# Grid decay matrices from one fp32r product per head, with the clamped difference on ScalarE

## The chip, the core and the metric

The kernel runs on one core of a Trainium2 chip. The metric is device time in microseconds (us) of one execution; lower is better. Before the change it is 1022.42 us, the median of 3 runs (1021.97 to 1022.79).

## The reference

Three blocks run over 256 tokens of width 1024: an attention block with an MLP, a second one, and a hybrid block in which neighbourhood attention on a grid (8 heads) and a bidirectional state-space scan (8 heads, chunks of 128 tokens) run side by side. The change lies in the scan. For each direction and head it needs

```
cum = jnp.cumsum(dtc * a.reshape(g, e), axis=2)
seg = cum[:, :, :, None] - cum[:, :, None, :]
lower = np.tril(np.ones((q, q), dtype=bool))[:, :, None, None]
decay = jnp.exp(jnp.where(lower, seg, -jnp.inf))
cb = jnp.einsum("bcign,bcjgn->bcijg", cc, bc)
m = cb[..., None] * decay * dtc[:, :, None]
y_diag = jnp.einsum("bcijge,bcjgep->bcigep", m, xc)
```

`seg` is at most 0 where the mask holds, so the kernel computes exp(min(seg, 0)) and lets the masked `cb` remove the rest.

## The kernel before

All instruction streams are written by hand, one program per engine, and are tied by semaphores. The dense products (helper `product`, L681 to L683) are three fp32r matmuls each, on weights that ScalarE (L1374, `split_hi`) and VectorE (L1904, `split_lo`) split into high and low parts.

The change touches the grid stage, some 70 us long. There TensorE runs the list of `grid_order`, 16 window steps i (head i // 2, token half i % 2), with these pieces:

- S(i), L1216: the logits of step i in one of four small banks. VectorE adds the bias and takes the maximum (`window_logits`, L2561), ScalarE takes the exponential (L1763), VectorE scales by the reciprocal of the sum (`window_normalise`, L2567 and L2570).
- P(i), L690: four transposes of the probabilities; ScalarE copies them out (L1374, work<-bank 128x512). O(h), L1233: probabilities times values. After two heads ScalarE copies the pair's output (`pair_out`, acts<-bank 128x256), and VectorE makes its low part (`pair_lo`, L2574).
- G(h), L1239: head h's cumulative sums broadcast to 128 rows, into the segment bank, by a selector column of `ident` repeated 128 times against `cum_rows`, two fp32 products of 256 columns (one for each direction).
- `decay(h)`, L2591: VectorE makes min(row - column, 0) in four pieces (256, 128, 128 and 256 columns) from the segment bank into E[h % 2]. ScalarE takes the exponential of its 768 columns (L1769). `matrix(h)`, L2605: VectorE multiplies by dt and `cb`. GpSimd adds the overlapping parts (L657). Y(h), L1263, is the product with the values.
- F(n), L1252: the carried state's rows, also in the segment bank, read by `carried_rows` (L2619, L2623). K(1), L1246: transposed keys, in that bank too, copied out by ScalarE at step 2.

The one segment bank goes round in the order of SEGMENTS (G0 G1 K1 F0 G2 G3 F1 G4 G5 F2 G6 G7 F3), and each of these waits on `seg_free` of the one before. Each engine walks the 16 steps:

```
TensorE step i:  P(i), segments of step i, S(i+3), Y, O
ScalarE step i:  exp of S(i); exp of E if i-1 in DECAY; copy of P(i-1)
VectorE step i:  logits(i); normalise(i-1); carried rows; decay if i in DECAY; matrix if i-1 in DECAY
```

with DECAY = (1, 2, 4, 5, 7, 8, 10, 11). G(h) is issued two steps before its decay. After step 15 come the first product of the output projection, O(7), and the transposes T of the scan's rows. In step 12 (ScalarE) and 13 (VectorE) one weight chunk is split as well.

Before the stage, L1126 to L1130 compute the cumulative sums of all 16 rows (2 directions x 8 heads) in one bank, VectorE copies them to `cum` (L2507), and four transposes (L1137) give the columns in `stat` (L2511).

Of the kernel before, what the change touches and what calls it, by code (L numbers as in the profile page):

```python
# [215 lines left out]
def program(nc, weights, x_in, ctx_in, cols_in, rows_in, consts_in, pos_col_in, t5_pos_in, t5_cols_in, rpb_in, c_dram,  # L216
            final_dram, t5_dram, out):
    with ExitStack() as stack:
# [20 lines left out]
        posc = sbuf("posc", [P, 2], I32)  # L239
        post = sbuf("post", [P, 448], I32)  # L240
        t5c = sbuf("t5c", [P, 66])
        posf = sbuf("posf", [P, 2])
        rot = sbuf("rot", [P, 2, 2, 32])
        adac = sbuf("adac", [P, 80])
# [59 lines left out]
        cxsr = view(arena, 10752, 2, NA)  # L304
        Bcr = view(arena, 11776, 2, 2, P)
        cbm = view(arena, 12288, 2, 768)
        cum, cum_rows = arena[0:16, 13824:14336], arena[:, 13824:14336]
        tmp = lambda k: arena[:, 12288 + 64 * k:12352 + 64 * k]
        E = (work[:, 0:768], arena[:, 0:768])
        Wm = view(arena, 10752, 2, 768)  # L310
# [77 lines left out]
        conv_mid, conv_act = sem("conv_centre"), sem("conv_activated")  # L388
        sp_abs, sp_exp, sp_u, sp_ln = (sem("softplus_" + n) for n in ("abs", "exp", "one_plus", "ln"))
        a_exp, dA_ready, ecum_ready = sem("a_exp"), sem("dA_ready"), sem("exp_cum")  # L390
        xw_ready, seg_exp = sem("xw_ready"), sem("seg_exp")
        seg_ready, seg_free = sem("segment_ready"), sem("segment_free")
        y_ready, y_free = sem("state_rows_ready"), sem("state_rows_free")
# [50 lines left out]
        def window_unit(kind, i):  # L444
# [2 lines left out]

        seg_bank, y_banks, pair_bank = (gbank(GU["out"]), (gbank(GU["out"] + 1), gbank(GU["out"] + 2)),
                                        gbank(GU["out"] + 3))

        def segment_out(eng, kind, i):
            eng.wait_ge(seg_ready, SEGMENTS.index((kind, i)) + 1)
# [150 lines left out]
        @block.gpsimd  # L603
        def _(pool):

            pool.memset(half[:, :], -0.5).then_inc(pool_step, 1)
            pool.wait_ge(pool_step, 1)
            pool.memset(bias[:, 4096:4352], 0.0).then_inc(bias_zeros, 1)

            def roots(first, last):  # L610
                for n in range(first, last):
                    a, b = ROOTS[n]
                    pool.wait_ge(means_ready, n + 1)
                    pool.tensor_tensor(stat[:, a:b], stat[:, a:b], half[:, 0:b - a], ALU.pow).then_inc(roots_ready, 1)  # L614

            def ada_load(j, land):

                u = j % 2
                pool.dma_start(land[:, 2048 * u:2048 * u + 2048], weights["ada"][j]).then_inc(ada_in[u], 16)

            roots(0, 3)
            pool.wait_ge(roots_ready, 3)
            pool.memset(kpT[0][64:128], 0.0).then_inc(kpe_zeros, 1)
            pool.wait_ge(kpe_zeros, 1)
            pool.memset(kpT[1][0:64], 0.0).then_inc(kpe_zeros, 1)
            pool.wait_ge(kpe_zeros, 2)
            roots(3, 7)

            pool.wait_ge(act_lo, LO0["mlp0"] + 1)
            for j in range(2):  # L630
                ada_load(j, att)
            roots(7, 8)
            for j in range(2, 10):
                pool.wait_ge(ada_used, j - 1)
                ada_load(j, att)
            roots(8, 11)

            pool.wait_ge(act_lo, LO0["mlp1"] + 1)
            for j in (10, 11):
                ada_load(j, bias)  # L640
            roots(11, 12)
            for j in range(12, 24):
                pool.wait_ge(ada_used, j - 1)
                ada_load(j, bias)
            roots(12, 14)
            pool.memset(cum_rows, 0.0).then_inc(zeros_ready, 1)
            pool.wait_ge(zeros_ready, 1)
            pool.memset(nqT[0][64:128], 0.0).then_inc(zeros_ready, 1)
            pool.wait_ge(zeros_ready, 2)
            small_out(pool, SU["cb"] + 1)  # L650
            pool.memset(nqT[1][0:64], 0.0).then_inc(zeros_ready, 1)
            pool.wait_ge(zeros_ready, 3)
            for h in range(H):
                pool.wait_ge(w_mat, h + 1)
                diagonal, other = (bass.AP(Wm.tensor, Wm.offset + 768 * (h % 2) + a, [list(Wm.ap[0]), [256, 2], [1, P]])
                                   for a in (0, 384))
                pool.tensor_tensor(diagonal, diagonal, other, ALU.add).then_inc(w_summed, 1)  # L657
            roots(14, len(ROOTS))
# [3 lines left out]
        def _(pe):  # L662
# [457 lines left out]
            def cumulative():  # L1120

                pe.wait_ge(dA_ready, 1)
                u = SU["cum"]
                small_start(u)
                b = sbank(u)
                pe.matmul(b[0:16, 0:T], dA(0), const("upto"), start=True, stop=False)  # L1126
                pe.matmul(b[0:16, P:T], dA(1), const("upto", 0, P), start=False, stop=True)
                pe.matmul(b[0:16, T:2 * T], dA(1), const("since"), start=True, stop=False)
                pe.matmul(b[0:16, T:T + P], dA(0), const("since", P, P), start=False, stop=True).then_inc(small_ready, 1)

            def cumulative_columns():

                small_gone(pe, SU["cum"])
                u = SU["cumcol"]
                small_start(u)
                for n in range(4):
                    ins = pe.transpose(sbank(u)[:, 16 * n:16 * n + 16], cum[:, P * n:P * n + P], ident[0:16, 0:16])  # L1137
                ins.then_inc(small_ready, 1)
                u = SU["later"]
                small_start(u)  # L1140
                b = sbank(u)
                for n, (parts) in enumerate((
                        [("after", 0), ("ones", 1)], [("before", 0)], [("after", 1)], [("before", 1), ("ones", 0)])):
                    for m, (tri, t) in enumerate(parts):
                        ins = pe.matmul(b[:, 16 * n:16 * n + 16], const(tri), dA(2 + t), start=m == 0,
                                        stop=m == len(parts) - 1)
                ins.then_inc(small_ready, 1)
# [60 lines left out]
            def grid_work(kind, i):  # L1208
# [26 lines left out]
                        ins.then_inc(pair_ready, 1)  # L1235
                elif kind == "G":
                    segment_start(kind, i)
                    for d in range(2):
                        ins = pe.matmul(seg_bank[:, d * T:(d + 1) * T], repeated(ident, 8 * d + i, P),  # L1239
                                        cum_rows[:, d * T:(d + 1) * T], start=True, stop=True)  # L1240
                    ins.then_inc(seg_ready, 1)
                elif kind == "K":
                    segment_start(kind, i)
                    pe.wait_ge(nqk_ready, 3)
# [119 lines left out]
        def _(act):  # L1364
# [354 lines left out]
            used(GC["q"])  # L1719
            used(GC["q"] + 1)  # L1720
            small_gone(act, SU["cumcol"])
            act.activation(stat[:, 320:384], stat[:, 256:320], ACT.Exp).then_inc(ecum_ready, 1)
            u = SU["later"]
            small_out(act, u)
            act.activation(tmp(7), sbank(u)[:, 0:64], ACT.Exp).then_inc(small_free[u % 4], 1)
# [33 lines left out]
            for i in range(2 * H + 1):  # L1759
                if i < 2 * H:  # L1760
# [2 lines left out]
                    act.activation(att[:, 1024 + 512 * (i % 2):1536 + 512 * (i % 2)], sbank(u)[:, :], ACT.Exp, scale=-1.0,  # L1763
                                   bias=stat[:, 56 + i % 2:57 + i % 2], accum_out=stat[:, 60 + i % 2:61 + i % 2])\
                        .then_inc(small_free[u % 4], 1)
                if i - 1 in DECAY:
                    h = DECAY.index(i - 1)
                    act.wait_ge(seg_free, SEGMENTS.index(("G", h)) + 1)
                    act.activation(E[h % 2], E[h % 2], ACT.Exp).then_inc(seg_exp, 1)  # L1769
                if i == 1:  # L1770
                    context_keys(1)
                if i == 14:
# [78 lines left out]
        def _(v):  # L1851
# [652 lines left out]

            u = SU["cum"]
            small_out(v, u)
            v.tensor_copy(cum, sbank(u)[0:16, :]).then_inc(small_free[u % 4], 1)  # L2507
            used(GC["q"])
            u = SU["cumcol"]
            small_out(v, u)  # L2510
            v.tensor_copy(stat[:, 256:320], sbank(u)[:, 0:64]).then_inc(small_free[u % 4], 1)  # L2511
            used(GC["q"] + 1)
            rotate(0)
            rotate(1)
# [60 lines left out]
                                acts[:, 1, 0, p * T:(p + 1) * T].bitcast(F32), ALU.subtract)\  # L2575
                    .then_inc(pair_free, 1)

            parts = ((0, 256, 0, 0), (256, 384, 128, 1), (384, 512, 256, 0), (512, 768, 256, 1))

            def decay(h):  # L2580

                segment_out(v, "G", h)
                if h == 0:
                    for g in range(2):
                        small_gone(v, SU["cb"] + g)
                    small_gone(v, SU["cumcol"])
                if h >= 2:
                    v.wait_ge(w_mat, h - 1)
                for n, (a, e, src, t) in enumerate(parts):
                    c = 256 + 16 * t + h if n < 2 else 256 + 32 + 16 * t + 8 + h  # L2590
                    ins = v.tensor_scalar(E[h % 2][:, a:e], seg_bank[:, src:src + e - a], stat[:, c:c + 1], 0.0,  # L2591
                                          ALU.subtract, ALU.min)
                    if n == 3:
                        ins.then_inc(seg_free, 1)
                    else:
                        step(ins)
                settle()

            def matrix(h):
                v.wait_ge(seg_exp, h + 1)  # L2600
                if h >= 2:
                    v.wait_ge(y_used, h - 1)
                for n, (a, e, src, t) in enumerate(parts):
# [8 lines left out]
            def carried_rows(n):  # L2612
# [2 lines left out]
                tm = arena[:, 1024:1536]  # L2615
                v.wait_ge(ecum_ready, 1)
                segment_out(v, "F", n)
                c = 320 + 32 * d + 16 * t + 8 * d
                v.tensor_tensor(heads(tm), heads(seg_bank[:, :]), spread(stat[:, c:c + 8], 1, 64), ALU.mult)\  # L2619
                    .then_inc(seg_free, 1)  # L2620
                v.wait_ge(seg_free, SEGMENTS.index(("F", n)) + 1)
# [31 lines left out]
            for i in range(2 * H + 1):  # L2653
# [3 lines left out]
                    window_normalise(i - 1)  # L2657
                if i % 3 == 0 and 3 <= i <= 12:
                    carried_rows(i // 3 - 1)
                if i in DECAY:  # L2660
                    decay(DECAY.index(i))
                if i - 1 in DECAY:
                    matrix(DECAY.index(i - 1))
                if i == 13:
# [285 lines left out]
```

## Time and profile before

| what | value |
|---|---|
| median of 3 runs | 1022.42 us |
| profiled execution, first to last instruction | 1021.6 us |
| TensorE busy, whole span | 990.6 us (97%) |
| VectorE busy | 696.0 us (68%) |
| ScalarE busy | 512.6 us (50%) |
| mean granted TensorE clock | 0.996 |

The profiled execution is told by its span, 1021.6 us; the device time has a little more around it (0.8 us against the median). Times in the profile are counted from the span's start. The grid stage runs from 728.9 us (the first S) to about 800.9 us (the transposes T).

### The profile page before, as it was taken

Reading aid. Unit: us, or ns where it says so; the run is one execution under the profiler, and the core shown is the slowest. Engines: PE = TensorE matmul, PEld = TensorE weight load, DVE = VectorE, ACT = ScalarE, POOL = GpSimd, SP = SyncE. Lnnn points to the kernel's source line nnn. Section 1 sums busy time; section 2 is a strip of 40 time slices with the busy share of each in tenths; the row PEclk is TensorE's granted clock in tenths of the full one; section 3 lists DMA queues with packets and bytes.
Section 4 is the critical chain, followed back from the end, with each engine's and each line's share of the span. In section 5 each row is a group of like instructions: output and inputs, shape, how many; then the busy total and the mean of one; then the engine's idle time right before and its main releaser. Section 6 shows DMA issues by size and latency. Waiting matters only on the chain. (4 is left out here: it accounts for less than half of the span.)

```text
span 1021.6 us, 15144 instructions
## 1 busy us (share of the span) xinstructions
PE 990.6 (97%) x5976; PEld 860.0 (84%) x5976; DVE 696.0 (68%) x996; ACT 512.6 (50%) x687; POOL 48.3 (5%) x61
## 2 busy tenths in 40 slices
PE   7999999999989999999999999999998989999997
PEld 5577899999978877899998988988865779999996
DVE  5776647777775665657778564456598587777775
ACT  2366474544545665545454463544445354444443
POOL 0220000000000110000001010000010000000000
PEclk9999999999999999999999999999999999999999
DMA  9035576667664533568887543234101245545541
GB/s 363 16 101 147 206 278 222 249 249 277 230 223 141 192 122 115 215 250 326 293 326 285 211 163 115 92 124 165 42 1 42 104 164 192 185 185 184 187 177 42
DMA packets 29727, 183.92 MB, mean 180 GB/s; under 512 B 3440, under 2 KB 6128, under 8 KB 10096
## 3 DMA queue, kind: packets, MB, share of 16 engines
q1 hardware_dynamic: 25360, 157.56, 43.0%
q0 software_dynamic: 3456, 25.17, 6.7%
q8 instruction: 32, 0.52, 0.2%
q10 hardware_dynamic: 864, 0.55, 0.2%
q14 instruction: 15, 0.12, 0.0%
HBM read 180.64 MB, written 2.62 MB: 179 GB/s over the span
## 5 line engine op out<-in xcount | busy, mean ns | idle before, releaser
L1904 DVE TENSOR_TENSOR split<-raw,split 128x2048 fp32r<-128x2048 f32 (+1 forms) x123 | 279.9, 2275 | 203.5 <-ACT split L1374 202.2
L1374 ACT ACTIVATE split<-raw 128x2048 fp32r<-128x2048 f32 x122 | 231.8, 1900 | 248.3 <-PE bank L683 219.0
L681 PE MATMUL bank<-acts,split 128*128 128x256 f32 (+1 forms) x1024 | 290.8, 284 | 2.3 <-DVE acts L1944 1.4
L683 PE MATMUL bank<-acts,split 128*128 128x256 f32 (+1 forms) x1024 | 289.7, 283 | 0.0
L682 PE MATMUL bank<-acts,split 128*128 128x256 f32 (+1 forms) x1024 | 289.6, 283 | 0.0
L681 PE MATMUL bank<-split,acts 128*128 128x512 f32 (+1 forms) x544 | 211.4, 389 | 0.6 <-DVE split L1904 0.4
L682 PE MATMUL bank<-split,acts 128*128 128x512 f32 (+1 forms) x544 | 209.3, 385 | 0.0
L683 PE MATMUL bank<-split,acts 128*128 128x512 f32 (+1 forms) x544 | 209.1, 384 | 0.0
L681 PEld LDWEIGHTS bank<-acts,split 128*128 128x128 f32 (+1 forms) x1024 | 194.7, 190 | 6.0 <-DVE split L1904 1.9
L682 PEld LDWEIGHTS bank<-acts,split 128*128 128x128 f32 (+1 forms) x1024 | 194.7, 190 | 2.5 <-issue 0.2
L683 PEld LDWEIGHTS bank<-acts,split 128*128 128x128 f32 (+1 forms) x1024 | 194.7, 190 | 0.4
L683 PEld LDWEIGHTS bank<-split,acts 128*128 128x128 f32 x544 | 102.7, 189 | 20.5
L681 PEld LDWEIGHTS bank<-split,acts 128*128 128x128 f32 x544 | 102.7, 189 | 20.5 <-issue 1.0
L682 PEld LDWEIGHTS bank<-split,acts 128*128 128x128 f32 x544 | 102.9, 189 | 18.5
L1374 ACT ACTIVATE acts<-arena 128x1024 fp32r<-128x1024 f32 (+2 forms) x76 | 50.6, 689 | 47.8 <-DVE arena L2736 46.6
L614 POOL TENSOR_TENSOR stat<-stat,half 128x2 f32<-128x2 f32 (+4 forms) x18 | 25.4, 1409 | 435.4 <-DVE stat L1860 435.4
L2290 DVE CUSTOM_DVE_ANT_0 arena<-work,arena 128x1024 f32<-128x1024 f32 x36 | 43.9, 1220 | 0.7
L2290 DVE CUSTOM_DVE_ANT_0 arena<-bias,arena 128x1024 f32<-128x1024 f32 x28 | 34.2, 1221 | 1.0 <-DVE stat L1892 0.2
L681 PE MATMUL bank<-acts 128*128 128x512 f32 x88 | 34.6, 393 | 0.2 <-DVE acts L2697 0.2
L1821 ACT ACTIVATE arena<-bank,cols 128x256 f32<-128x256 f32 x22 | 12.4, 564 | 44.1 <-PE bank L683 44.1
L682 PE MATMUL bank<-acts 128*128 128x512 f32 x88 | 34.5, 392 | 0.0
L683 PE MATMUL bank<-acts 128*128 128x512 f32 x88 | 34.2, 389 | 0.0
(250 smaller groups left out, 1065.8 us busy)
## 6 DMA issues: line engine op xcount, KB each, us to landing
raw<-w_mlp SPq DMA_DIRECT2D x64, 1024.0 KB, 4.8
raw<-w_glu SPq DMA_DIRECT2D x22, 1024.0 KB, 4.8
bias<-w_ada POOLq DMA_DIRECT2D x14, 1024.0 KB, 6.8
raw<-w_qkv SPq DMA_DIRECT2D x12, 1024.0 KB, 4.7
arena<-w_glu_down SPq DMA_DIRECT2D x22, 512.0 KB, 3.3
work<-w_ada POOLq DMA_DIRECT2D x10, 1024.0 KB, 7.0
raw<-w_mla_o SPq DMA_DIRECT2D x4, 1024.0 KB, 5.8
raw<-w_moba_o SPq DMA_DIRECT2D x4, 1024.0 KB, 4.8
```

The source lines that it names most:

```text
L614: pool.tensor_tensor(stat[:, a:b], stat[:, a:b], half[:, 0:b - a], ALU.pow).then_inc(roots_ready, 1)
L681: pe.matmul(out_, a[0], b[0], start=first, stop=False)
L682: pe.matmul(out_, a[0], b[1], start=False, stop=False)
L683: return pe.matmul(out_, a[1], b[0], start=False, stop=last)
L1374: return act.activation(out_, in_, ACT.Copy)
L1821: act.activation(gact[:, b, :], gbank(u)[:, 0:T], ACT.Identity, scale=w, bias=bb).then_inc(glu_mid, 1)
L1904: v.tensor_tensor(split[:, c % 2, 1, 0:n], raw[:, c % 2, 0:n], split[:, c % 2, 0, 0:n].bitcast(F32), ALU.subtract).then_inc(lo_ready, 1)
L2290: ins = v.tensor_tensor_reduce(out=ada_junk[:, t, :], accum_out=modr[:, f:f + 1], scale=1.0, scalar=0.0, in0=(bias if layer else att)[:, 2 ...
```

## The change

Four things change. The 16 rows of cumulative sums become 8 rows with both directions in one row: columns 0 to 255 forward, 256 to 511 backward. The sums are split for fp32r: `cumr` rows 0 to 7 hold the rounded value, rows 32 to 39 what is left, and `pick` has ones at both places, so that one fp32r product of 512 columns adds the two and broadcasts a head's row. The clamped difference moves from VectorE to ScalarE, as Relu(column - row) in the same four pieces, and the exponential has scale -1. It moves from behind VectorE's normalise to behind ScalarE's exponential of the same step, and the exponential of E follows at once instead of one step later. VectorE's `decay` is gone.

```diff
-                pe.matmul(b[0:16, 0:T], dA(0), const("upto"), start=True, stop=False)
+                pe.matmul(b[0:8, 0:T], dA(0)[:, 0:8], const("upto"), start=True, stop=False)
...
-                    ins = pe.transpose(sbank(u)[:, 16 * n:16 * n + 16], cum[:, P * n:P * n + P], ident[0:16, 0:16])
+                    ins = pe.transpose(sbank(u)[:, 8 * n:8 * n + 8], cum[0:8, P * n:P * n + P], ident[0:8, 0:8])
...
                 elif kind == "G":
                     segment_start(kind, i)
-                    for d in range(2):
-                        ins = pe.matmul(seg_bank[:, d * T:(d + 1) * T], repeated(ident, 8 * d + i, P),
-                                        cum_rows[:, d * T:(d + 1) * T], start=True, stop=True)
-                    ins.then_inc(seg_ready, 1)
+                    if i == 0:
+                        pe.wait_ge(cum_parts, 1)
+                    pe.matmul(seg_bank[:, :], repeated(pick[:, :], i, P), cumr[:, :], start=True, stop=True)\
+                        .then_inc(seg_ready, 1)
...
-                if i - 1 in DECAY:
-                    h = DECAY.index(i - 1)
+                if i in DECAY:
+                    h = DECAY.index(i)
+                    segment_out(act, "G", h)
+                    if h >= 2:
+                        act.wait_ge(w_mat, h - 1)
+                    for n, (a, e, src, t) in enumerate(parts):
+                        c = 256 + 8 * t + h + 16 * (n // 2)
+                        ins = act.activation(E[h % 2][:, a:e], seg_bank[:, src:src + e - a], ACT.Relu, scale=-1.0,
+                                             bias=stat[:, c:c + 1])
+                    ins.then_inc(seg_free, 1)
                     act.wait_ge(seg_free, SEGMENTS.index(("G", h)) + 1)
-                    act.activation(E[h % 2], E[h % 2], ACT.Exp).then_inc(seg_exp, 1)
+                    act.activation(E[h % 2], E[h % 2], ACT.Exp, scale=-1.0).then_inc(seg_exp, 1)
...
-            v.tensor_copy(cum, sbank(u)[0:16, :]).then_inc(small_free[u % 4], 1)
+            v.tensor_copy(cum[0:8], sbank(u)[0:8, :]).then_inc(small_free[u % 4], 1)
+            small_gone(v, u)
+            step(v.tensor_tensor(pick[:, :], ident[:, 0:8], ident[:, 32:40], ALU.add))
+            step(v.tensor_copy(cumr[0:8, :], cum[0:8]))
+            settle()
+            v.tensor_tensor(cumr[32:40, :], cum[0:8], cumr[0:8, :].bitcast(F32), ALU.subtract).then_inc(cum_parts, 1)
...
-            def decay(h):
...
-                if i in DECAY:
-                    decay(DECAY.index(i))
```

ScalarE's order of instructions at steps 4 and 5, before (L1763 is the window's exponential, L1769 that of E, L1374 the copy of P):

```order
L1763 ACTIVATE work,stat<-bank,stat 128x512 [waits max_ready]
L1374 ACTIVATE work<-bank 128x4x128 [waits small_ready]
L1763 ACTIVATE work,stat<-bank,stat 128x512 [waits max_ready]
L1769 ACTIVATE work<-work 128x768 [waits segment_free]
L1374 ACTIVATE work<-bank 128x4x128 [waits small_ready]
```

The same steps now (L1769 is the window's exponential, L1779 the Relu pieces, L1783 the exponential of E, L1380 the copy):

```order
L1769 ACTIVATE work,stat<-bank,stat 128x512 [waits max_ready]
L1779 ACTIVATE work<-bank,stat 128x256 [waits mask_matrix_ready,segment_ready]
L1779 ACTIVATE work<-bank,stat 128x128 x2
L1779 ACTIVATE work<-bank,stat 128x256
L1783 ACTIVATE work<-work 128x768 [waits segment_free]
L1380 ACTIVATE work<-bank 128x4x128 [waits small_ready]
L1769 ACTIVATE work,stat<-bank,stat 128x512 [waits max_ready]
L1779 ACTIVATE arena<-bank,stat 128x256 [waits mask_matrix_ready,segment_ready]
```

Four Relu pieces and the exponential of E now stand between the window's exponential and the copy of the step before, in both steps.

TensorE's order at steps 3 and 4, before (L690 is P, L1239 is G, L1216 is S, L1263 is Y, L1252 is F):

```order
L1239 MATMUL bank<-arena,consts 128x256 [waits segment_free]
L1239 MATMUL bank<-arena,consts 128x256
L1216 MATMUL bank<-arena 128x512 [waits small_free0]
L1263 MATMUL bank<-arena 128x64 [waits mask_diagonals_summed]
L1263 MATMUL bank<-arena 128x64 x3
L690 MATMUL bank<-consts,work 128x128 [waits small_free1,probs_ready]
L690 MATMUL bank<-consts,work 128x128 x3
L1252 MATMUL bank<-work,arena 128x256 [waits segment_free]
```

The G of the same place now, and the S behind it:

```order
L1246 MATMUL bank<-cumr,pick 128x512 [waits segment_free]
L1222 MATMUL bank<-arena 128x512 [waits small_free0]
```

Two fp32 products became one of fp32r; nothing else of TensorE's order moved, and F(1) still waits for the segment bank that G(3) filled.

## Rows read from the trace of the kernel before

**Rows 1.** The page: busy us of each engine, its share of the span, instructions.

```profile
PE 990.6 (97%) x5976; PEld 860.0 (84%) x5976; DVE 696.0 (68%) x996; ACT 512.6 (50%) x687; POOL 48.3 (5%) x61
```

**Rows 2.** Window: busy us of PE, PEld, DVE, ACT, POOL; granted clock; DMA.

```profile
740.00:790.00 50.00, 46.23 (x233) 31.33 (x231) 44.10 (x125) 25.70 (x52) 5.81 (x8) 1.00 0.05 16
```

**Rows 3.** Waits of TensorE in 727 to 803 us: us in total, times, longest.

```profile
PE bank L690 <- DVE work L2570: 1.2, 2, 1.0
PE bank L1252 <- ACT arena L1374: 0.7, 1, 0.7
PE bank L1252 <- DVE arena L2591: 0.6, 1, 0.6
PE bank L1239 <- DVE work L2591: 0.6, 1, 0.6
PE bank L1216 <- ACT work L1763: 0.6, 1, 0.6
```

**Rows 4.** Timeline of TensorE: start us, us of the group, what, count.

```profile
744.62 1.03 PE L1239 MATMUL bank<-arena,consts 128*128 128x256 f32 x4
745.48 1.02 PE L1216 MATMUL bank<-arena 128*128 128x512 f32 x2
...
798.19 0.39 PE L681 MATMUL bank<-split,acts 128*128 128x512 f32 x1
798.42 0.39 PE L682 MATMUL bank<-split,acts 128*128 128x512 f32 x1
```

**Rows 5.** Timeline of VectorE where the sums are copied (684 to 690 us).

```profile
685.00 0.67 DVE L2507 COPY arena<-bank 16x512 f32<-16x512 f32 x1
687.37 2.29 DVE L1904 TENSOR_TENSOR split<-raw,split 128x2048 fp32r<-128x2048 f32 x1 [1.70 <-ACT split L1374]
```

**Rows 6.** ScalarE: three costs from PSUM (timeline, groups by form, timeline).

```profile
802.94 1.55 ACT L1375 ACTIVATE acts<-bank,cols 128x256 fp32r<-128x256 f32 x4
...
L1374 ACT ACTIVATE acts<-bank 128x256 fp32r<-128x256 f32 x4 | 1.5, 381 | 3.5 <-PE bank L1233 3.5
...
680.84 1.00 ACT L1713 ACTIVATE arena<-bank,cols 128x256 f32<-128x256 f32 x2
```

**Rows 7.** ScalarE: a line's durations in ns, min/median/max; L1763 has the bias as a column.

```profile
L1375 ACT ACTIVATE acts<-bank,cols x4: 456/471/482, 802.9 to 804.0; 128x256 fp32r<-128x256 f32 x4
...
L1763 ACT ACTIVATE work<-bank,stat x16: 678/687/691, 731.3 to 789.9; 128x512 f32<-128x512 f32 x16
```

**Rows 8.** Timeline of ScalarE around step 10.

```profile
767.39 0.84 ACT L1769 ACTIVATE arena<-arena 128x768 f32<-128x768 f32 x1
...
770.61 0.69 ACT L1763 ACTIVATE work<-bank,stat 128x512 f32<-128x512 f32 x1 [1.61 <-DVE stat L2561]
...
773.42 0.60 ACT L1374 ACTIVATE work<-bank 128x512 f32<-128x512 f32 x1 [2.03 <-PE bank L690]
```

**Rows 9.** The chain that ended last, 755 to 763 us: start us, us, what.

```profile
756.40 0.60 PE bank L690 x4
...
757.03 0.60 ACT work L1374
757.62 0.28 ACT acts L1374
...
757.93 0.43 DVE acts L2574
758.36 0.61 DVE bank L2561
...
759.48 1.39 DVE work L2591 x4
...
760.92 1.13 PE bank L1239 x4
```

**Rows 10.** Timeline of TensorE at the stage's end: P(15), and the transposes T.

```profile
792.85 0.66 PE L690 MATMUL bank<-consts,work 128*128 128x128 f32 x4
...
800.92 1.03 PE L690 MATMUL bank<-consts,work 128*128 128x128 f32 x8
```

More of the change, by code:

```diff
@@ L241, in program @@
         t5c = sbuf("t5c", [P, 66])
+        cumr = sbuf("cumr", [P, 512], F32R)
+        pick = sbuf("pick", [P, 8], F32R)
         posf = sbuf("posf", [P, 2])
@@ L306, in program @@
         cbm = view(arena, 12288, 2, 768)
-        cum, cum_rows = arena[0:16, 13824:14336], arena[:, 13824:14336]
+        cum = arena[0:16, 13824:14336]
         tmp = lambda k: arena[:, 12288 + 64 * k:12352 + 64 * k]
@@ L390, in program @@
         a_exp, dA_ready, ecum_ready = sem("a_exp"), sem("dA_ready"), sem("exp_cum")
+        cum_parts = sem("cum_parts_ready")
         xw_ready, seg_exp = sem("xw_ready"), sem("seg_exp")
@@ L449, in program @@
                                         gbank(GU["out"] + 3))
+        parts = ((0, 256, 0, 0), (256, 384, 128, 1), (384, 512, 256, 0), (512, 768, 256, 1))
         def segment_out(eng, kind, i):
@@ L645, in _ @@
             roots(12, 14)
-            pool.memset(cum_rows, 0.0).then_inc(zeros_ready, 1)
+            pool.memset(cumr[:, :].bitcast(F32), 0.0).then_inc(zeros_ready, 1)
             pool.wait_ge(zeros_ready, 1)
@@ L1125, in cumulative @@
                 b = sbank(u)
-                pe.matmul(b[0:16, 0:T], dA(0), const("upto"), start=True, stop=False)
-                pe.matmul(b[0:16, P:T], dA(1), const("upto", 0, P), start=False, stop=True)
-                pe.matmul(b[0:16, T:2 * T], dA(1), const("since"), start=True, stop=False)
-                pe.matmul(b[0:16, T:T + P], dA(0), const("since", P, P), start=False, stop=True).then_inc(small_ready, 1)
+                pe.matmul(b[0:8, 0:T], dA(0)[:, 0:8], const("upto"), start=True, stop=False)
+                pe.matmul(b[0:8, P:T], dA(1)[:, 0:8], const("upto", 0, P), start=False, stop=True)
+                pe.matmul(b[0:8, T:2 * T], dA(1)[:, 8:16], const("since"), start=True, stop=False)
+                pe.matmul(b[0:8, T:T + P], dA(0)[:, 8:16], const("since", P, P), start=False, stop=True)\
+                    .then_inc(small_ready, 1)
             def cumulative_columns():
@@ L1721, in _ @@
             small_gone(act, SU["cumcol"])
-            act.activation(stat[:, 320:384], stat[:, 256:320], ACT.Exp).then_inc(ecum_ready, 1)
+            act.activation(stat[:, 320:352], stat[:, 256:288], ACT.Exp).then_inc(ecum_ready, 1)
             u = SU["later"]
@@ L2510, in _ @@
             small_out(v, u)
-            v.tensor_copy(stat[:, 256:320], sbank(u)[:, 0:64]).then_inc(small_free[u % 4], 1)
+            v.tensor_copy(stat[:, 256:288], sbank(u)[:, 0:32]).then_inc(small_free[u % 4], 1)
             used(GC["q"] + 1)
@@ L2576, in pair_lo, with matrix @@
                     .then_inc(pair_free, 1)
-            parts = ((0, 256, 0, 0), (256, 384, 128, 1), (384, 512, 256, 0), (512, 768, 256, 1))
-            def decay(h):
-                segment_out(v, "G", h)
+            def matrix(h):
+                v.wait_ge(seg_exp, h + 1)
                 if h == 0:
@@ L2585, in decay @@
                         small_gone(v, SU["cb"] + g)
[L2586 to L2600, printed above, removed]
                 if h >= 2:
@@ L2617, in carried_rows @@
                 segment_out(v, "F", n)
-                c = 320 + 32 * d + 16 * t + 8 * d
+                c = 320 + 16 * d + 8 * t
                 v.tensor_tensor(heads(tm), heads(seg_bank[:, :]), spread(stat[:, c:c + 8], 1, 64), ALU.mult)\
```

## The prediction

> **What bounds the kernel now.** I read the page first: TensorE is busy for 990.6 of 1021.6 us [rows 1], so a saving must end up on TensorE's own path. Then the window of the stage that the change touches: in 50 us TensorE is busy for 46.2, VectorE for 44.1, ScalarE for 25.7 [rows 2]. So the stage is bound by TensorE with VectorE close behind, and ScalarE looks half free. Then TensorE's waits there: F(0) 0.7, F(3) 0.6 and G(5) 0.6 us for the segment bank, P(12) and P(14) 1.2 for the normalise, S(15) 0.6 for an exponential [rows 3]. They are short, but they show that the loop TensorE to ScalarE to VectorE and back takes about as long as TensorE's own work. Last the chain of waits from P(5) on [rows 9]: it leaves TensorE for ScalarE's copy, `pair_out`, VectorE's `pair_lo`, logits and decay, and comes back with G(5) at 760.92 us. This loop decides the case.
>
> **TensorE's term.** G is four passes: 744.62 to 745.48 us, 0.86 us [rows 4] (a group's first start to the next one's, since matmuls overlap). The new G is one pass of 512 fp32r columns; such products start 0.23 us apart [rows 4]. Eight heads give 8 x (0.86 - 0.23) = 5.0 us less on TensorE. This is the best that the edit can do.
>
> **VectorE's and ScalarE's terms.** VectorE loses eight decays of 1.39 us [rows 9], 11.1 us. ScalarE gains 32 Relu pieces, read from PSUM, with a column as bias; no row of before has this form. A 128x512 one with a bias column takes 687 ns from PSUM, one of 128x256 with a scale column 471 [rows 7]; the difference of 216 for 256 columns is 0.84 ns per column, so a piece of 128 columns takes about 365 ns. Back to back, four of 256 columns take 1.55 us, so they start (1.55 - 0.47) / 3 = 0.36 us apart [rows 6, 7], and 128 columns 0.26. I take 0.37 and 0.27 for the semaphores around them: 2 x 0.37 + 2 x 0.27 = 1.28 us per head, 10.2 us in all. From below: a copy without any column takes 0.38 us for 256 columns, of which 0.10 overlaps [rows 6], so 0.28 and 0.17, 0.90 per head. From above: with two columns (L1713) a pair takes 1.00 us [rows 6], 0.45 apart if one lasts 0.55; with 0.35 for 128 columns 1.60 per head; with no overlap at all 0.56 and 0.45, 2.02.
>
> The Trainium skill speaks against this move: its page ScalarE: Activation LUTs, section Rules for kernel authors, gives relu and add to VectorE. In the same page, section What ACT_TABLE_LOAD costs, a piece with a pointer operand takes 280 ns plus 0.833 ns a column and back-to-back ones overlap by 93 ns: an estimate of 0.40 and 0.29, 1.38 per head, by which the schedule below ends at +0.3 us where mine ends at -0.3.
>
> **What hides, and what does not.** I laid the four instruction orders side by side from 728.9 us on, by arithmetic: an instruction starts when its engine is free and 0.04 us after its last releaser ends. Occupancies from the timeline: S, F and G 0.86, P 0.44, Y 0.88, O 2.02 with its change of shape, window exponential 0.67, exponential of E 0.74, copies 0.49, logits 0.61, reciprocal and scaling 0.60, decay and matrix 1.31, and 0.11 for TensorE after a stall. For the kernel before this puts P(15) at 793.1 and T at 801.1, where the trace has 792.85 and 800.92 [rows 10], and gives the waits of rows 3 to within 0.2 us each. Then I made the change in it. Its waits, before and now:
>
> - K(1) 0.3 to 1.3 and F(0) 0.8 to 1.3: Relu(1) stands behind the exponential of step 2, and the copy of K behind Relu(1), the exponential of E and the copy of P(1).
> - F(1) 0 to 0.9: the bank is G(3)'s until Relu(3). From the exponential of step 4 ScalarE now does 0.67 + 1.28 + 0.13 + 0.74 + 0.49 + 0.67 + 1.28, 5.3 us in a row. TensorE's three savings by then are gone: F(1) starts at 752.6, as before.
> - P(6) 0.2 to 0.8: the chain from P(5) [rows 9], copy, `pair_out`, `pair_lo`, logits(7), normalise(6), is unchanged at some 3.2 us, and beside it TensorE has 3.0 us of work before and 2.4 now. The saving of G(4) turns into a wait one for one. G(5) 0.8 to 1.0.
> - P(10) 0.2 to 1.4: the exponential of step 10 starts at 770.6 [rows 8], since logits(10) stand behind carried rows and a matrix. Relu and the exponential of E fill ScalarE for 2.2 us after it, so the copy of P(9) starts at about 773.2, where it now starts at 773.42 [rows 8], released by TensorE. F(3) 0.8 to 1.0.
> - S(15) 0.7 to 1.1, P(12) 0.4 to 0: the split chunk on ScalarE at step 12 stands as before. P(14) stays.
>
> The waits grow by 1.0 + 0.5 + 0.9 + 0.6 + 0.3 + 1.2 + 0.2 + 0.5 - 0.4 = 4.8 us, some 0.1 more at G(3) and G(7). Against 5.0 us that leaves -0.1 to -0.2 with pieces of 0.38 and 0.27 us, and **-0.3 us** at my 1.28 per head. Each 0.1 us per head on the four pieces moves the end by 0.6 us.
>
> **Edits that I cost at nothing.** VectorE's three new instructions at the sums (8 columns, then 512 twice, each at most the 0.67 of the copy) are some 1.5 us behind L2507, where VectorE is idle for 1.70 us until ScalarE's split [rows 5]; without that cover they would push one split chunk by 1.5 us. Eight output rows in place of 16, transposes of 8 rows, 32 columns copied instead of 64: the same instruction counts, under 0.1 us. The memset has the same size and place. No ACT_TABLE_LOAD is added in the new order. SP's and GpSimd's orders do not change.
>
> **The forecast.** -0.3 us on a profiled span of 1021.6, so 1021.3; the median stands 0.8 above the span, and on 1022.42 it gives **1022.1 us**. A measurement of this kernel can tell about 0.2%, 2.0 us, from no change.
>
> **Rivals.**
> - *TensorE stays the bound.* The short waits of before do not grow, VectorE's 11.1 us were what paced the loop, and the 5.0 us are kept: 1017.4. For it: TensorE is busy for 92% of the window, VectorE for 88% [rows 2]. Against it: P(6)'s chain has no decay in it. A half-way case has Relu pieces at the lower bound of 0.90 per head: -2.6, 1019.8. Together 0.15.
> - *ScalarE becomes the bound.* Place: steps 4-5, 7-8 and 10-11, where two heads follow each other and the copy of P and the next window exponential queue behind 2.2 us of new work. At 1.60 per head the schedule gives +1.6, at 1.80 +2.8, at 2.02 +4.2 (1026.6). It is slower than noise from 1.67 per head on. For it: two columns cost 0.45 apart [rows 6]. Against it: one column costs 0.36. 0.14, and in this I count that the granted clock, 1.00 (2.4 GHz) in this window [rows 2] with waits up to 1.0 us, might fall with longer ones.
> - *The product does not get cheap.* If the new G still took 0.86, the schedule gives +1.3: 1023.7. It costs little because the loop waits anyway. It lies within no change; of the 0.71 there, 0.05.
>
> **Numbers.** Forecast case 0.66, product 0.05, faster cases 0.15, slower 0.14: faster 0.15, same 0.71, slower 0.14. The forecast's own bounds (1.10 to 1.60 per head, -1.4 to +1.6) are 1021.0 to 1024.0; the range goes on to the half-way case and half of the slower one: 1019.2 to 1025.2.
>
> **What would show it.** G one instruction at about 0.23 us to the next start; the Relu pieces 0.37 and 0.27 us apart; VectorE's busy time down by about 10 us and ScalarE's up by 10 to 13; TensorE's busy time in the stage down by 5 and its waits up by nearly as much, now with F(1), P(6) and P(10) at about 1 us each, released by ScalarE or the normalise; T within 0.5 us of 800.9. The prediction is wrong if P(10) and F(1) do not wait, or if the Relu pieces are more than 0.1 us off.

## The result and the profile after

| kernel | executions | median, us | from to | ratio, 95% interval |
|---|---|---|---|---|
| before | 20 | 1022.79 | 1021.83 to 1023.85 | |
| changed | 20 | 1024.62 | 1022.41 to 1028.44 | 1.0017 (1.0011 to 1.0023) |

The changed kernel is slower by 0.17%, 1.8 us: within what I had called no change and inside the range, but on the other side of it from my -0.3 us, and the interval excludes a gain. The executions of the changed kernel are also spread over 6.0 us, against 2.0 before, and the spread goes with TensorE's granted clock: eight have a mean clock of 0.997 over the span and took 1022.41 to 1023.86 us, nine have 0.992 to 0.994 and took 1025.19 to 1028.44; three stand at 0.995 (1023.83 to 1024.72). The profiled execution is one of the longer ones: 1024.2 us of span (1025.95 us of device time), 2.6 more than before's 1021.6.

Device time and span don't differ by the same amount in all kernels. In every execution with both on record it is 2.07 to 2.21 us where VectorE makes the clamped difference, and 1.74 to 1.94 us where ScalarE makes it; why is open. So 1.8 us more of device time are about 2.1 us more of span.

Busy time on the page of the changed kernel, with the granted clock in 40 slices (compare [rows 1]):

```profile
PE 989.2 (97%) x5952; PEld 857.0 (84%) x5952; DVE 687.3 (67%) x967; ACT 522.2 (51%) x719; POOL 48.3 (5%) x61
PEclk9999999999999999999999999999989999999999
```

VectorE lost 8.7 us (10 expected) and ScalarE gained 9.6 (10 to 13 expected). But one digit of the clock is an 8, in the slice that holds 762 us.

TensorE's waits in the grid stage of the changed kernel, 727 to 805 us (us in total, times, longest; L695 is P, L1258 F, L1252 K, L1222 S, L1246 G):

```profile
PE bank L695 <- DVE work L2589: 2.8, 3, 1.1
PE bank L1258 <- ACT arena L1779: 1.5, 2, 0.9
PE bank L1258 <- ACT arena L1380: 1.2, 1, 1.2
PE bank L1252 <- ACT arena L1779: 1.1, 1, 1.1
PE bank L1222 <- ACT work L1769: 1.0, 1, 1.0
PE bank L1246 <- ACT work L1779: 0.9, 1, 0.9
```

They sum to 8.5 us where [rows 3] and a shorter one beside them (K(1), 0.2) made 3.9. Six of nine are now released by ScalarE. The growth is 4.6 us, where the side-by-side schedule gave 4.8.

The TensorE timeline of the changed kernel around two of these waits (start, duration, instruction, idle time before it):

```profile
740.23 0.66 PE L1252 MATMUL bank<-consts,arena 128*128 128x128 f32 x4 [1.11 <-ACT arena L1779]
742.07 1.13 PE L1258 MATMUL bank<-work,arena 128*128 128x256 f32 x4 [1.19 <-ACT arena L1380]
744.26 0.48 PE L1246 MATMUL bank<-cumr,pick 128*128 128x512 f32 x1
744.57 1.02 PE L1222 MATMUL bank<-arena 128*128 128x512 f32 x2
...
759.18 0.66 PE L695 MATMUL bank<-consts,work 128*128 128x128 f32 x4 [0.70 <-DVE work L2589]
760.69 0.50 PE L1246 MATMUL bank<-cumr,pick 128*128 128x512 f32 x1 [0.85 <-ACT work L1779]
...
764.20 3.68 PE L1239 MATMUL bank<-work,arena 128*64 128x256 f32 x8
```

G is one product with 0.31 us to the next start (744.26 to 744.57), where it was 0.86; the eight bring some 4.4 of the 5.0 us. G(5) starts at 760.69, 0.23 us earlier than before's 760.92 [rows 9]; but the stage itself began 0.45 us earlier (first S at 728.42, before at 728.87), so that within the stage G(5) is 0.22 us later. Up to here the forecast holds: the waits have eaten the saving. The next O (L1239) then takes 3.68 us, where the same eight products took 1.94 before. The windows show why (us, busy time of TensorE, its weight loads, VectorE, ScalarE and GpSimd with instruction counts, granted clock, DMA):

```profile
757.00:760.00 3.00, 2.13 (x14) 1.47 (x12) 2.43 (x9) 1.84 (x7) 0.00 (x0) 1.00 0.00 0
760.00:762.00 2.00, 1.31 (x3) 0.82 (x4) 0.79 (x3) 1.97 (x6) 0.00 (x0) 0.82 0.01 4
762.00:764.00 2.00, 2.00 (x9) 1.53 (x7) 1.96 (x8) 1.97 (x7) 0.73 (x1) 0.50 0.00 0
764.00:766.00 2.00, 2.00 (x7) 1.09 (x7) 0.16 (x1) 0.78 (x1) 0.00 (x0) 0.50 0.00 0
766.00:768.00 2.00, 2.00 (x6) 0.85 (x5) 0.00 (x0) 0.00 (x0) 0.00 (x0) 0.50 0.00 0
768.00:770.00 2.00, 2.00 (x10) 1.52 (x10) 0.44 (x1) 1.26 (x3) 0.00 (x0) 0.97 0.00 0
740.00:790.00 50.00, 43.44 (x201) 28.26 (x202) 30.65 (x84) 30.75 (x71) 5.09 (x7) 0.93 0.00 1
```

From 757 to 762 us TensorE was busy for 3.44 us of 5. Then its granted clock was 0.50 (1.2 GHz instead of 2.4) for about seven microseconds, in which it was never idle. P(8) starts at 770.15, 2.4 us later than before's 767.76. From G(5) to P(8) 9.46 us pass; in a second profile of the same kernel, shown below, where the clock stays at 1.00 here, it is 6.21. So this fall cost 3.25 us. Before, no microsecond of 738 to 790 is under 0.99.

The waits alone are not why the changed kernel is slower: they only eat its saving. What makes it slower is the clock. That a fall follows from the waits is what the experiments have to show.

### The profile page after: what moved, and what is told of

It is laid out like the page before. It is cut to its first block and busy times, and to the rows that moved or that the text cites. A ratio compares the mean times of both kernels' runs of the same rounds, so it can differ in the third digit from the quotient of the medians.

```text
span 1024.2 us, 15094 instructions
## 1 busy us (share of the span) xinstructions
PE 989.2 (97%) x5952; PEld 857.0 (84%) x5952; DVE 687.3 (67%) x967; ACT 522.2 (51%) x719; POOL 48.3 (5%) x61
## 5 line engine op out<-in xcount | busy, mean ns | idle before, releaser
L1380 ACT ACTIVATE split<-raw 128x2048 fp32r<-128x2048 f32 x122 | 231.8, 1900 | 247.8 <-PE bank L688 239.3
L1380 ACT ACTIVATE acts<-arena 128x1024 fp32r<-128x1024 f32 (+2 forms) x76 | 50.6, 689 | 48.1 <-DVE arena L2735 46.9
L686 PE MATMUL bank<-acts 128*128 128x512 f32 x88 | 34.6, 393 | 0.2 <-DVE acts L2696 0.2
L687 PE MATMUL bank<-acts 128*128 128x512 f32 x88 | 34.5, 392 | 0.0
L695 PEld LDWEIGHTS bank<-consts,work 128*128 128x128 f32 x192 | 21.9, 143 | 15.0 <-issue 5.9
```

The costliest lines, as they stand in the source:

```text
L686: pe.matmul(out_, a[0], b[0], start=first, stop=False)
L687: pe.matmul(out_, a[0], b[1], start=False, stop=False)
L695: ins = pe.transpose((gbank if large else sbank)(u)[0:m, at:at + k], src, ident[0:k, 0:k])
L1380: return act.activation(out_, in_, ACT.Copy)
```

## The experiments

**Two theories.** *Clock*: the Relu pieces turn the product's saving into waits, and in a part of the executions these make the clock fall; without the fall the change would be level or a little faster. *ScalarE*: the longer loop through ScalarE is itself the cost, and the clock an accident.

**Each half alone.** First the product alone, with the decay back on VectorE (fewer waits):

```diff
-                if i in DECAY:
-                    h = DECAY.index(i)
...
+                if i - 1 in DECAY:
+                    h = DECAY.index(i - 1)
...
+                    ins = v.tensor_scalar(E[h % 2][:, a:e], seg_bank[:, src:src + e - a], stat[:, c:c + 1], 0.0,
+                                          ALU.subtract, ALU.min)
```

> The one fp32r product and the split sums as in the change, but the clamped difference stays on VectorE and the exponential of E one step later, as before. Theory A (the Relu pieces on ScalarE are what eats the saving; side-by-side schedule): P(6) and P(10) still wait 0.8 us, F(1) not at all, T is 3.5 us earlier than before, so 1019.3 us. Theory B (TensorE's saving always turns into waits and a lower granted clock, wherever the difference is made): no gain beyond 1 us, and a stretch with the granted clock at 0.50 in some executions.

Measured: 1020.39 us (7 executions, 1019.21 to 1020.72) beside 1022.85 for the kernel before (31 executions), ratio 0.9974 (0.9963 to 0.9984). So 2.5 us are kept: more than the 1 us that theory B allows, and 1.0 less than the 3.5 of theory A. Every execution has a clock of 0.996 or more. TensorE's waits, 727 to 805 us:

```profile
PE bank L695 <- DVE work L2581: 2.5, 4, 1.0
PE bank L1258 <- ACT arena L1380: 0.7, 1, 0.7
PE bank L1246 <- DVE work L2598: 0.6, 1, 0.6
PE bank L1258 <- DVE arena L2598: 0.6, 1, 0.6
PE bank L1222 <- ACT work L1769: 0.6, 1, 0.6
PE bank L1252 <- DVE arena L2598: 0.2, 1, 0.2
```

They sum to 5.2: 1.3 more than before, where the full change has 4.6 more. Then the Relu pieces alone, with the two fp32 products of before:

```diff
-                if i - 1 in DECAY:
+                if i in DECAY:
...
+                        ins = act.activation(E[h % 2][:, a:e], seg_bank[:, src:src + e - a], ACT.Relu, scale=-1.0,
+                                             bias=stat[:, c:c + 1])
...
-            def decay(h):
```

> The kernel before with only the clamped difference moved to ScalarE (G stays two fp32 products, 0.86 us). Theory A: the schedule gives +1.1 to +1.3 us, 1024.0, with TensorE as busy as before, so no execution with a lower clock and a spread of runs as narrow as before. If moving the difference cost nothing by itself, it would be at 1022.8.

Measured: 1023.71 us (11 executions, 1023.04 to 1025.65), ratio 1.0009 (1.0000 to 1.0018). One execution of eleven had a clock under 0.996 (0.994, 1025.65 us), where none was expected. It has the long waits at F(0), S(15) and P(14), 1.0 to 1.2 us each, but K(1), 1.8 us ahead of F(0), waits for only 0.5. In span the difference is 1.2 us (medians of 1021.9 and 1020.7), as the schedule gave. The two halves give -2.5 and +0.9, together -1.6, and the change gives +1.8. Of the 3.4 us between, the side-by-side schedule explains 2.0 at full clock (-3.5 and +1.2 for the halves, -0.3 together: with the late releases the product's saving turns into waits). The other 1.4 us are in no schedule at full clock.

**Filling the waits.** In the changed kernel TensorE makes 36 more of the same fp32r products just ahead of its waits, into banks whose next use overwrites them. They are extra work whose results nobody reads.

```diff
+            FILL = {('P', 1): 5, ('F', 0): 5, ('P', 4): 4, ('P', 6): 6, ('P', 10): 8, ('P', 12): 4, ('P', 14): 4}
+                for _ in range(FILL.get((kind, i), 0)):
+                    pe.matmul(bank[:, :], repeated(pick[:, :], 0, P), cumr[:, :], start=True, stop=True)
...
                 elif kind == "P":
+                    small_start(window_unit(kind, i))
+                    filler(sbank(window_unit(kind, i)), kind, i)
                     pe.wait_ge(probs_ready, 2 * H + i + 1)
```

> The changed kernel with 36 extra fp32r products of 512 columns into banks that are free at that moment, set where TensorE waits (before P1, F0, P4, P6, P10, P12, P14), 8.3 us of added TensorE work whose results are overwritten. Theory clock: the granted clock is 1.00 throughout the grid stage in every execution, the runs above 1025 us are gone, and the median is 1022.5 to 1023.3, faster than the changed kernel by 1.5 us although it does more. Theory without the clock: the extra work costs 0 to 2 us on top of 1024.6.

Measured: 1022.13 us (11 executions, 1021.68 to 1022.94), ratio 0.9993 (0.9984 to 1.0002). More work made the changed kernel 2.5 us faster in the median, and its spread shrank from 6.0 to 1.3 us, with every clock from 0.996 to 0.998. That is a little more than the clock theory expected (1022.5 to 1023.3), and against the other theory, which had the extra work cost up to 2 us. Waits of 727 to 805 us, and the window 740 to 790:

```profile
PE bank L1254 <- ACT work L1791: 0.3, 1, 0.3
PE bank L1270 <- ACT arena L1791: 0.3, 1, 0.3
...
740.00:790.00 50.00, 49.28 (x245) 33.23 (x244) 34.19 (x92) 32.70 (x76) 5.10 (x7) 1.00 0.06 22
```

ScalarE does the same 32 Relu pieces in the same places, and TensorE's pieces start no earlier than their releasers allow. Only TensorE's idle time is gone. That decides for the clock: ScalarE's loop is the same in both kernels. A rival is that TensorE needs about 0.1 us to start again after a wait, at seven places 0.7 us at most, and that the filling gives this back. The stage table further down speaks against it: at full clock the stage takes as long with the filling as without.

**A longer product instead of filling.** Each G of the change is made four times:

```diff
-                    pe.matmul(seg_bank[:, :], repeated(pick[:, :], i, P), cumr[:, :], start=True, stop=True)\
-                        .then_inc(seg_ready, 1)
+                    for _ in range(4):
+                        ins = pe.matmul(seg_bank[:, :], repeated(pick[:, :], i, P), cumr[:, :], start=True, stop=True)
+                    ins.then_inc(seg_ready, 1)
```

> The changed kernel with each head's product made four times over (0.92 us instead of 0.23, about what G took before). Theory clock: TensorE is again as busy as before, no fall of the clock, time as in the Relu-alone run, near 1024.1 and narrow. Theory without the clock: 1024.6 plus 1.6, 1026.2.

Measured: 1024.29 us (12 executions, 1023.48 to 1027.06), ratio 1.0019 (1.0010 to 1.0027). Three of twelve executions have clocks of 0.994 or 0.995 (1026.18 to 1027.06); the other nine have a median of 1024.15, against 1023.36 for the eight executions of the change at 0.997. So G's three more products, some 5.5 us over the eight heads, cost 0.8 us against these eight, and nothing in the median over all. The clock theory had expected no execution to fall, and three of twelve did; these are the ones over 1025 us, and whether they are fewer than in the change (nine of twenty) can't be told from so few. Busy time elsewhere does not help as filling at the waits does: F(0), S(15) and P(14) still wait for 1.0 to 1.2 us, and K(1) for 0.4.

**The change once more.** A single profiled execution of the changed kernel.

> The changed kernel once more, for a second profile. Clock theory: either a granted clock of 1.00 in all of 727 to 803 us and a span of 1020.5 to 1022.0, or one stretch at 0.50 of some 7 us and a span above 1023.5; the waits of TensorE are the same in both to within 0.1 us each outside that stretch.

Measured: 1023.32 us, span 1021.5, clock 0.997, with the same six groups of waits (F's in sum 0.4 shorter). Neither of the expected cases came: there is a fall, but a short one and at another place:

```profile
740.00:742.00 2.00, 0.81 (x6) 0.55 (x5) 0.00 (x0) 2.00 (x4) 0.00 (x0) 1.00 0.00 0
742.00:743.00 1.00, 1.00 (x4) 0.80 (x3) 0.00 (x0) 0.25 (x2) 0.00 (x0) 0.59 0.00 0
743.00:745.00 2.00, 2.00 (x5) 0.86 (x4) 1.65 (x3) 0.00 (x0) 0.00 (x0) 0.50 0.00 0
745.00:746.00 1.00, 1.00 (x6) 0.95 (x5) 1.00 (x5) 0.22 (x1) 0.00 (x0) 0.70 0.00 0
...
760.00:762.00 2.00, 1.14 (x6) 0.72 (x6) 0.93 (x4) 1.97 (x6) 0.00 (x0) 1.00 0.00 0
762.00:768.00 6.00, 6.00 (x33) 4.11 (x32) 3.59 (x10) 4.67 (x12) 0.73 (x1) 1.00 0.00 1
```

TensorE was busy for 0.81 of 2 us, through the waits of K(1) and F(0), and the clock was at or near 0.50 for about 3.4 us afterwards. In this execution F(0) to G(2) took 3.79 us, in the first profile 2.19: the fall cost 1.6 us. The wait of F(1) then shrank from 0.63 to 0.23 us, so by F(1) 1.1 us of it were left (F(0) started 0.44 earlier, F(1) 0.64 later). And where the first profile fell, nothing did. Two microseconds up to the start of F(0) and two up to the start of G(5), in the first profile and then in this one, are alike:

```profile
740.07:742.07 2.00, 0.66 (x4) 0.42 (x4) 0.00 (x0) 1.97 (x5) 0.00 (x0) 1.00 0.00 0
758.69:760.69 2.00, 0.66 (x5) 0.42 (x5) 1.60 (x5) 1.97 (x7) 0.00 (x0) 1.00 0.00 0
...
739.63:741.63 2.00, 0.66 (x4) 0.42 (x4) 0.00 (x0) 1.97 (x5) 0.00 (x0) 1.00 0.00 0
759.33:761.33 2.00, 0.66 (x4) 0.42 (x4) 1.60 (x5) 1.97 (x7) 0.00 (x0) 1.00 0.00 0
```

TensorE was busy for 0.66 of 2 us in all four, and the clock fell after the second and the third of them alone. So the same program with the same waits falls in one place or the other, briefly or for longer.

The mean clock of a span is a poor sign of this. A value of 0.997 does not mean that an execution had no fall, and a low one need not come from this stage. The kernel before falls too, elsewhere, behind waits of 1.08 and 1.70 us (starts at 301.04 and 305.84):

```profile
306.00:308.00 2.00, 1.85 (x9) 1.38 (x9) 1.90 (x4) 1.97 (x3) 0.00 (x0) 0.85 0.03 8
308.00:310.00 2.00, 2.00 (x7) 1.52 (x6) 1.97 (x3) 2.00 (x8) 0.00 (x0) 0.50 0.00 0
```

Seven of the ten profiles have a fall at this place, the first of the change too, which so had two. This profile and those of G made four times and of the late filling have none there.

**The stage at full clock.** Where the stage starts differs by up to 1.4 us between the profiles, so its length is the better measure, from the start of the first S to that of T:

| profile | first S | G(5) | T | first S to T | lowest clock in it |
|---|---|---|---|---|---|
| before | 728.87 | 760.92 | 800.92 | 72.05 | 1.00 |
| changed, first | 728.42 | 760.69 | 803.47 | 75.05 | 0.50, behind G(5) |
| changed, second | 727.97 | 761.33 | 800.87 | 72.90 | 0.50, ahead of G(5) |
| product alone | 728.54 | 758.59 | 797.51 | 68.97 | 1.00 |
| pieces alone | 728.74 | 761.80 | 801.95 | 73.21 | 1.00 |
| 36 products more | 727.84 | 760.18 | 799.67 | 71.83 | 1.00 |
| G four times | 728.05 | 761.29 | 801.58 | 73.53 | 1.00 |

The changed kernel ran at 1.00 up to G(5) in its first profile (32.27 us) and from G(5) on in its second (39.54 us). Put together that is a stage of 71.81 us without a fall: 0.24 us less than before, where -0.3 was forecast, and as long as the filled one. So the filling gives back the falls and nothing else that can be seen.

**Which waits.** The 36 products cut into the early ones (P(1), F(0), P(4), P(6): 20) and the late ones (P(10), P(12), P(14): 16).

```diff
-            FILL = {('P', 1): 5, ('F', 0): 5, ('P', 4): 4, ('P', 6): 6, ('P', 10): 8, ('P', 12): 4, ('P', 14): 4}
+            FILL = {('P', 1): 5, ('F', 0): 5, ('P', 4): 4, ('P', 6): 6}
```

> The changed kernel with the fill before P1, F0, P4 and P6 alone (20 products), which is all before the place where the granted clock fell in the profile of the change (761 us). Clock theory: no execution falls there; the waits at P10, F3, S15 and P14 are left, so a fall there stays possible. If the early waits bring the fall, the runs above 1025 us are gone and the median is 1022.3 to 1023.0; if any of the waits can bring it, a part of the runs stays above 1025.

> The changed kernel with the fill before P10, P12 and P14 alone (16 products), all behind 761 us. If the early waits bring the fall, half of the runs stay above 1024.5 and the profile may show it near 761 us; the median stays near 1024.3.

Measured, early: 1023.50 us (11 executions, 1021.42 to 1024.49), ratio 1.0005 (0.9996 to 1.0014), all clocks 0.996 or more; the median is 0.5 us above what was expected. Late: 1023.29 us (12 executions, 1021.09 to 1026.77), ratio 1.0010 (1.0000 to 1.0021), five of twelve over 1024.5, four of these with clocks of 0.993 to 0.995; its profile shows the fall after F(0) again, 0.50 from 743 to 745, and not the one near 761. Filling the early waits takes away the executions above 1024.5 us (none of eleven) and the low clocks, and filling the late ones leaves them (five of twelve): the longest executions hang on the early waits. But the early filling's median is no better than the late one's. Its executions form two groups, four at 1021.42 to 1021.91 and seven at 1023.41 to 1024.49, and the seven do not have the lower clocks (0.997 all, where the four have 0.996 or 0.998). The late waits (P(10), F(3), S(15) and P(14), 4.0 us together in its profile) are the only thing that this kernel has and the full filling, without such a second group, has not. That they bring the second group is argued; its only profile is of the shorter group and shows no fall in the stage, which takes 71.87 us.

**The better version.** The product alone with 19 extra products at P(1), F(0), P(6), P(10), P(12) and P(14):

```diff
+            FILL = {('P', 1): 2, ('F', 0): 3, ('P', 6): 4, ('P', 10): 4, ('P', 12): 2, ('P', 14): 4}
```

> The G-alone kernel (difference on VectorE) with 19 extra fp32r products where its TensorE waits are. G alone was at 1020.4 us with no execution of a clock under 0.996. Theory: what the fill gives is the restart of TensorE after a stall (about 0.1 us each, some six stalls) and a safe clock; so 1019.5 to 1020.0. If the fill stands in the way of a copy or a segment anywhere, slower than 1020.4.

Measured: **1019.73 us** (9 executions, 1019.22 to 1020.44) beside 1022.85 (27 executions), ratio 0.9971 (0.9961 to 0.9980). It is 3.1 us faster than before and 4.9 faster than the change. Against the product alone (1020.39 on another chip) the 0.7 us are not certain, and the profiles don't show them: the stage takes 68.98 us with the extra products and 68.97 without, and ran at 1.00 in both. So the time is the expected one, but the reason given for it, the restart after a wait, is not borne out. What is shown to be better is the product alone. The waits left are the three that the extra products do not cover:

```profile
PE bank L1254 <- DVE work L2610: 0.6, 1, 0.6
PE bank L1228 <- ACT work L1781: 0.5, 1, 0.5
PE bank L1270 <- DVE arena L2610: 0.5, 1, 0.5
```

## Why the prediction was right up to the sum and wrong in its sign

**TensorE's term: right, a little large.** The next start comes 0.31 us after G's, not 0.23, because a following product of another kind starts later than one of the same kind. Eight make 4.4 us.

**ScalarE's term: right.** The pieces in the changed kernel, by form (busy time, mean ns), and one group of steps 4 and 5 on ScalarE's timeline:

```profile
L1779 ACT ACTIVATE arena<-bank,stat 128x256 f32<-128x256 f32 x8 | 3.9, 485 | 0.0
L1779 ACT ACTIVATE arena<-bank,stat 128x128 f32<-128x128 f32 x8 | 2.5, 378 | 0.0
...
750.03 0.68 ACT L1769 ACTIVATE work<-bank,stat 128x512 f32<-128x512 f32 x1
750.69 1.35 ACT L1779 ACTIVATE arena<-bank,stat 128x256 f32<-128x256 f32 x4
752.08 0.84 ACT L1783 ACTIVATE arena<-arena 128x768 f32<-128x768 f32 x1
```

From the first piece to the exponential of E 1.39 us pass, against 1.28 + 0.13 = 1.41 in the forecast. The estimate from the Trainium skill's page ScalarE: Activation LUTs, section What ACT_TABLE_LOAD costs, would have been 1.38 + 0.13, a little too long: in the trace pieces of 485 and 378 ns start such that each overlaps the next by about 0.12 us. The advice against the move in the Trainium skill, the same page, section Rules for kernel authors, held here, by +0.9 us for the pieces alone.

**The waits: right.** Forecast and measured: K(1) 1.3 and 1.11, F(0) 1.3 and 1.19, F(1) 0.9 and 0.63, P(6) 0.8 and 0.70, G(5) 1.0 and 0.85, P(10) 1.4 and 1.10, F(3) 1.0 and 0.85, S(15) 1.1 and 1.01, P(12) gone in both, P(14) stays. The late start of F(1) holds (752.6; measured 752.10 in a stage that began 0.45 us earlier), and so do all the places. The schedule made the waits 0.1 to 0.3 us too long, and G 0.08 too short; these offset each other.

**The halves: right, the first a little large.** The same schedule gave -3.5 for the product alone and +1.2 for the pieces alone. In the stage they measure -3.1 and +1.2, in the medians of device time -2.5 and +0.9.

**VectorE's new instructions: hidden.** The work at the sums in the changed kernel:

```profile
685.29 0.17 DVE L2523 TENSOR_TENSOR pick<-consts 128x8 fp32r<-128x8 f32 x1
685.37 0.41 DVE L2524 CAST cumr<-arena 8x512 fp32r<-8x512 f32 x1
685.82 0.68 DVE L2526 TENSOR_TENSOR cumr<-arena,cumr 8x512 fp32r<-8x512 f32 x1
686.95 2.29 DVE L1918 TENSOR_TENSOR split<-raw,split 128x2048 fp32r<-128x2048 f32 x1 [0.46 <-ACT split L1380]
```

The split chunk still waits 0.46 us for ScalarE and starts at 686.95, not later than before's 687.37 [rows 5].

**The step that failed: the end was summed at full clock.** "5.0 less on TensorE, 4.8 more waiting, so -0.3" holds for a TensorE that runs at 1.00 throughout: put together from the stretches at 1.00, the stage is 0.24 us shorter, so the terms and the waits were right. But [rows 2, 3] show that clock only with waits that sum to 3.9 us over the stage. I had seen the possibility, but put it as a remark inside the ScalarE rival, with no price and no rows of its own; my sum counted a microsecond of waiting as worth exactly a microsecond. Measured, a fall added 1.6 us to 2.19 us of work in one profile and 3.25 to 6.21 in the other. It should have been a rival of its own: work that TensorE keeps after the waits takes twice as long until the clock is back, so 3.5 us at 0.50 cost some 1.7 us, and the likeliest case needed a chance for it near one half. T, which I put within 0.5 us of 800.9, stood at 803.47 in the first profile and at 800.87 in the second. The second is luck: its stage began 0.9 us earlier than before's, and what was left of its fall, 1.1 us, used that up.

What the Trainium skill says might have led there: its page TensorE: Matmul & The Clock Gate, section HAM oscillation — how this bites in real kernels, describes a kernel whose TensorE waits again and again between groups of products and loses its clock each time. The two falls here agree in kind, but not in size: the Trainium skill's kernel waited for DMA, about 3 to 5 us each time, and this one mostly for ScalarE, never over 1.2 us, and the clock fell all the same. By the length of its waits alone this kernel would have passed for safe; the measurement decides.

The rivals, as they stood, are out. That TensorE stays the bound is excluded: a half of the saving was kept only where the decay stayed on VectorE. That ScalarE becomes the bound by long pieces is excluded by the 1.39 us, 1.26 of them the pieces, where 1.67 was its condition. The product got cheap.

**What stays open.** Why one execution falls at 742 us and another at 761, and why one fall lasts twice as long as the other, was not settled: at K(1), F(0), P(6) and G(5) the two profiled executions have the same waits to 0.01 us. How many executions have no fall at all is not known either, since the mean clock does not show a short one and counts the fall near 306 us with it; the filled kernel and the shorter group of the early filling, 1021.4 to 1022.9 us, are the nearest to what the change would do without any.

## What to carry to other kernels

When a product is made cheap, follow its consumer: here the loop through ScalarE ate nearly all of the saving, and moving the clamped difference onto the engine that looked half free made that loop longer just where TensorE waits for it. Here the product alone, 2.5 us faster than before, was the better half. Do not book a wait on TensorE at its length alone; where waits of about a microsecond follow each other, look at the granted clock by windows of one or two microseconds, in more than one profile, and count the spread of the executions as evidence. If such waits can't be removed, spare products ahead of them are cheap to try: here 36 of them gave back 2.5 us, and 19 gave nothing that the profiles show where the clock had not fallen. Compare a stage by its length, not by the time at which it ends.

## What the runs showed of the hardware that was not expected

- Extra TensorE work made a TensorE-bound kernel faster: 1024.62 to 1022.13 us with 36 products of 512 columns, and the spread fell from 6.0 to 1.3 us.
- The granted clock can fall or stay after the same stretch of work in the same program: with TensorE busy for 0.66 of the last 2 us, it fell behind F(0) and stayed behind G(5) in one execution, and the other way round in another. While it was low, TensorE was busy without a gap, for about 3.4 and about 7 us, before it rose.
- The kernel before, too, has a fall at 306 to 311 us, down to 0.50, in a stretch that this change does not touch. Three of the ten profiles do not have it; in two of these the two waits ahead of it are the same, 1.08 and 1.70 us.
- A fall is swallowed only in part by the waits behind it. Of 1.6 us lost, 1.1 were left at F(1), the next wait. Of 3.25 us lost from G(5) to P(8) all were left at T, though P(10), F(3), S(15) and P(14) wait in between: their releasers had been late by as much.
